# Linear attention's root ahead of the first half's exponentials on ScalarE, its output ahead of the second half's maximum on VectorE

## The chip, the cores and the metric

The kernel runs on one core of one Trainium2 chip. The metric is the device time of one execution in microseconds (us); less is better. Of a kernel that is timed several times the median is given.

## The reference

One decoder layer: 1024 tokens, width 1024, batch 1, float32. One projection feeds two groups of heads; their outputs are joined, projected and added, and an MLP follows. The part that the change touches is the work on one block of 128 tokens:

```
# head group A: sliding window attention, 8 heads of 64
s = einsum(q, k2) * dh**-0.5 + bias            # 128 queries, 256 keys
m = max(max(s), sink);  p = exp(s - m)
p = p / (sum(p) + exp(sink - m));  o = p @ v2
# head group B: chunked gated linear attention, 4 heads, keys 64, values 128
A = where(causal, q_t @ k_t.T, 0)              # within a chunk of 64 tokens
o = A @ v + q_t @ S_prev;  S = decay * S + k_s.T @ v
o = rms_norm(o) * gla_norm_g;  gla = o * silu(g_out)
mix = concat([attn, gla]) @ w_out
```

## The kernel before

The program of each engine is written out by hand, in order, and semaphores tie them together; nothing reorders it. After the input projections comes the attention loop: 8 blocks of 128 tokens. Block 0 is written out, blocks 1 to 7 are the turns of a loop (`Fori(1, NT)` on VectorE, `Fori(1, NT - 1)` and one more `steady` on ScalarE, a Python loop on TensorE). The loop is pipelined: turn n makes scores and exponentials of block n and finishes attention and linear attention of block n - 1.

- TensorE (PE), turn n: `front(n, 0)` scores of heads 0 to 3 (L848); `probs_turned` twice, transposes of block n - 1's probabilities (L815); `front(n, 1)` scores of heads 4 to 7; `attend(n - 1)` (L826); first part of `g_out(n)`, 12 matmuls (L784); `gla_scores(n)` (L860); `out_turned(n - 1)`, which transposes `gla_out` (L834); `gla_keys(n)` (L869); second part of `g_out(n)`, 12 matmuls; `gla_out_of(n)`: products with keys (L893), with the mask `a_mask` (L902), with `state_a` and `state_b` (L913).
- VectorE (DVE), turn n: `scores(n, 0)`, which moves two score tiles out of PSUM (L1330) and takes maximum, negated maximum and sink difference (L1336 to L1338); `gla_variance` (L1375); `gla_next_state` (L1381); `scores(n, 1)`; `gla_finish`, a Newton step on the root (L1123 to L1126) and the four products that make `gla_out` (L1391); `normalise(n, 0)` (L1344, L1345 and four L1347); `mix_attn` and `mix_gla`, the low halves of the joined output (L1353); `gla_mask` (L1358); `normalise(n, 1)`; `gla_state_b` (L1366).
- ScalarE (ACT), turn n: `turned` twice (L1820, L1822); `gla_squares` (L1842); `sigmoid` (L1859); `exps(n, 0)`, four exponentials and one of the sinks (L1827, L1828); `gla_root`, logarithm and exponential of 4 columns (L1728, L1729); `mix_hi` of the attention part (L1836); `exps(n, 1)`; `mix_hi` of the linear attention part; `keys` (L1832); `silu_exp` (L1851 to L1854).
- GpSimd (POOL): after `silu_exp`, a low part (L585) and a sum (L588); after `sigmoid`, the product that makes the gate `silu_g` (L590), for which `gla_finish` waits.

The waits that matter: `exps(n, g)` waits for the sink difference of that half (semaphore `neg_max`), `gla_finish` for root and gate, `out_turned` for `gla_out`, the second `mix_hi` for `out_turned`, `mix_gla` for the second `mix_hi`, and `gla_out_of` for mask and keys. Nothing on the way has a second buffer that could take up a late step.

Of the kernel before, what the change touches and what calls it, by code (L numbers as in the profile page):

```python
# [152 lines left out]
def build(nc, x, c, w_ada, b_ada, w_in, w_gate_up, b_gate, gla_norm_g, attn_sinks, rel_bias,  # L153
# [222 lines left out]
    with block:  # L376
# [717 lines left out]
        def _(v):  # L1094
# [16 lines left out]
            def split_lo(s, par):  # L1111
                v.wait_ge(s_hi, s + 1)
                v.tensor_tensor(w_lo[:, par, :], raw[:, par, :], w_hi[:, par, :], ALU.subtract).then_inc(s_lo, 1)  # L1113
# [7 lines left out]
            def newton(y, vv, t):  # L1121

                own.link(v.tensor_tensor(t, y, y, ALU.mult))  # L1123
                own.link(v.tensor_tensor(t, t, vv, ALU.mult))
                own.link(v.tensor_scalar(t, t, -0.5, 1.5, ALU.mult, ALU.add))
                return v.tensor_tensor(y, y, t, ALU.mult)  # L1126
# [195 lines left out]
            def scores(n, g, first=False):  # L1322

                for j in range(2):
                    hp = 2 * g + j
                    v.wait_ge(s_sc_full, 4 * n + hp + 1)
                    if not first and j == 0:
                        v.wait_ge(s_pt_full, 4 * (n - 1) + 2 * g + 2)
                    lo = P if first else 0
                    v.scalar_tensor_tensor(prob[:, 2 * hp:2 * hp + 2, lo:256],  # L1330
                                           bank[hp % 2][:, :].rearrange("p (h k) -> p h k", h=2)[:, :, lo:256],
                                           DH ** -0.5, bias[:, 2 * hp:2 * hp + 2, lo:256], ALU.mult, ALU.add)\
                        .then_inc(s_sc_free, 1)
                h = slice(4 * g, 4 * g + 4)
                v.wait_ge(s_sc_free, 4 * n + 2 * g + 2)
                own.link(v.tensor_reduce(mx[:, h], prob[:, h, :], AX.X, ALU.max))  # L1336
                own.link(v.scalar_tensor_tensor(nm[:, h], mx[:, h], -1.0, n_sink[:, h], ALU.mult, ALU.min))
                v.tensor_tensor(sd[:, h], nm[:, h], n_sink[:, h], ALU.subtract).then_inc(s_nm, 1)  # L1338

            def normalise(n, g):  # L1340

                h = slice(4 * g, 4 * g + 4)
                v.wait_ge(s_exp, 2 * n + g + 1)
                own.link(v.tensor_tensor(den[:, h], rs[:, h], es[:, h], ALU.add))  # L1344
                own.link(v.reciprocal(den[:, h], den[:, h]))  # L1345
                for i in range(4 * g, 4 * g + 4):
                    ins = v.tensor_scalar(prob[:, i, :], prob[:, i, :], den[:, i:i + 1], None, ALU.mult)  # L1347
                ins.then_inc(s_pn, 1)
# [6 lines left out]
            def gla_mask(n):  # L1355

                for hh in range(2):
                    ins = v.copy_predicated(a_mask[:, hh:GLA_HEADS:2, :],  # L1358
                                            tri[:, :].bitcast(I32).unsqueeze(1).broadcast_to([P, 2, P]),
                                            bank[(5, 7)[hh]][:, 0:2 * P].rearrange("p (h q) -> p h q", h=2))  # L1360
                ins.then_inc(s_at, 1)

            def gla_state_b(n):
                v.wait_ge(s_ds_full, n + 1)
                for tt in range(2):
                    ins = v.scalar_tensor_tensor(state_b[:, tt, :], state_a[:, tt, :], dec(n, 0, tt),  # L1366
                                                 bank[5][:, tt * P:(tt + 1) * P], ALU.mult, ALU.add)
                ins.then_inc(s_st_b, 1)
# [4 lines left out]
            def gla_variance(n):  # L1373
                v.wait_ge(s_gsq, n + 1)
                v.tensor_scalar(gvar, gss, 1.0 / DV, EPS, ALU.mult, ALU.add).then_inc(s_gvar, 1)  # L1375

            def gla_next_state(n):

                v.wait_ge(s_st_b, n + 1)
                for tt in range(2):  # L1380
                    ins = v.scalar_tensor_tensor(state_a[:, tt, :], state_b[:, tt, :], dec(n, 1, tt),  # L1381
                                                 bank[7][:, tt * P:(tt + 1) * P], ALU.mult, ALU.add)
                ins.then_inc(s_st_a, 1)

            def gla_finish(n):

                v.wait_ge(s_sg, n + 1)
                v.wait_ge(s_grt, n + 1)
                own.link(newton(grs, gvar, gnt))
                for h in range(GLA_HEADS):  # L1390
                    ins = v.scalar_tensor_tensor(gla_out[:, h, :], bank[(6, 4)[h % 2]][:, h // 2 * P:(h // 2 + 1) * P],  # L1391
                                                 grs[:, h:h + 1], silu_g[:, h * DV:(h + 1) * DV], ALU.mult, ALU.mult)
                ins.then_inc(s_og, 1)

            def mix_attn(n):
                mix(act_lo[:, 0:4, ds(n * P, P)], act_hi[:, 0:4, ds(n * P, P)], bank[2], s_oa_hi, n + 1, s_oa_lo)

            def mix_gla(n):
                mix(act_lo[:, 4:8, ds(n * P, P)], act_hi[:, 4:8, ds(n * P, P)], bank[4], s_gt_hi, n + 1, s_gt_lo)

            scores(0, 0, first=True)
            split_lo(SLOT_T + 3, (SLOT_T + 1) % 2)
            scores(0, 1, first=True)
            v.wait_ge(s_at_full, 1)
            gla_mask(0)
            normalise(0, 0)
# [7 lines left out]
            with v.Fori(1, NT, 1) as n:  # L1414
                own.enter(n - 1, LINKS)
                scores(n, 0)
                gla_variance(n - 1)
                gla_next_state(n - 1)
                scores(n, 1)
                gla_finish(n - 1)  # L1420
                normalise(n, 0)
                mix_attn(n - 1)
                v.wait_ge(s_at_full, n + 1)
                mix_gla(n - 1)
                gla_mask(n)
                normalise(n, 1)
                gla_state_b(n)
                own.leave(NT - 1)
# [279 lines left out]
        def _(a):  # L1708
# [17 lines left out]
            def root(y, vv, t):  # L1726

                own.link(a.activation(t, vv, ACT.Ln))  # L1728
                return a.activation(y, t, ACT.Exp, scale=-0.5)  # L1729
# [87 lines left out]
            def turned(n, g):  # L1817

                a.wait_ge(s_pt_full, 4 * n + 2 * g + 1)
                a.activation(prob_t[:, g, 0, :], bank[2][:, :], ACT.Copy).then_inc(s_pt_2, 1)  # L1820
                a.wait_ge(s_pt_full, 4 * n + 2 * g + 2)
                a.activation(prob_t[:, g, 1, :], bank[3][:, :], ACT.Copy).then_inc(s_pt_3, 1)  # L1822

            def exps(n, g):
                a.wait_ge(s_nm, 2 * n + g + 1)
                for h in range(4 * g, 4 * g + 4):
                    a.activation(prob[:, h, :], prob[:, h, :], ACT.Exp, bias=nm[:, h:h + 1], accum_out=rs[:, h:h + 1])  # L1827
                a.activation(es[:, 4 * g:4 * g + 4], sd[:, 4 * g:4 * g + 4], ACT.Exp).then_inc(s_exp, 1)  # L1828
# [5 lines left out]
            def mix_hi(tiles, n, b, wait, done):  # L1834
                a.wait_ge(wait, n + 1)
                a.activation(act_hi[:, tiles, ds(n * P, P)], b[:, :].rearrange("p (t q) -> p t q", t=4), ACT.Copy)\  # L1836
                    .then_inc(done, 1)

            def gla_squares(n):
                a.wait_ge(s_go_full, n + 1)  # L1840
                for h in range(GLA_HEADS):
                    ins = a.activation(gla_out[:, h, :], bank[(6, 4)[h % 2]][:, h // 2 * P:(h // 2 + 1) * P],  # L1842
                                       ACT.Square, accum_out=gss[:, h:h + 1])
                ins.then_inc(s_gsq, 1)
# [11 lines left out]
            def sigmoid(n):  # L1856

                a.wait_ge(s_sg_sum, n + 1)
                a.activation(silu_g[:, :], silu_g[:, :], ACT.Exp, scale=-1.0).then_inc(s_sigmoid, 1)  # L1859

            def gla_root(n):
                a.wait_ge(s_gvar, n + 1)
                root(grs, gvar, gln).then_inc(s_grt, 1)
# [5 lines left out]
            def steady(n):  # L1869
                turned(n - 1, 0)  # L1870
                turned(n - 1, 1)
                gla_squares(n - 1)
                sigmoid(n - 1)
                exps(n, 0)
                gla_root(n - 1)
                mix_hi(slice(0, 4), n - 1, bank[2], s_oa_full, s_oa_hi)
                exps(n, 1)
                mix_hi(slice(4, 8), n - 1, bank[4], s_gt_full, s_gt_hi)
                keys(n)
# [244 lines left out]
```

## Time and profile before

| | before |
|---|---|
| median of 3 runs | 1111.54 us (1108.22 to 1111.82) |
| profiled execution, its own time | 1111.64 us |
| its span in the profile | 1109.5 us |
| TensorE busy | 1039.9 us, 94% |
| VectorE busy | 702.4 us, 63% |
| ScalarE busy | 462.9 us, 42% |
| GpSimd busy | 94.3 us, 8% |
| one turn of the loop, 302.14 to 319.22 | 17.08 us: TensorE 16.11 busy, VectorE 13.58, ScalarE 12.04, GpSimd 4.47 |

The span is the time from the first to the last instruction on the chip; the 2.1 us between it and the execution's time lie around it. Busy is the time in which at least one instruction of an engine runs. In the loop all engines hand work to one another within a turn, so that what counts is who waits for whom, and not the share alone. The granted clock of TensorE is 1.00 in the turn.

### The profile page before, as it was taken

What the parts mean: (1) busy time and instruction counts of PE and PEld (TensorE: products, weight loads), DVE (VectorE), ACT (ScalarE), POOL (GpSimd) and SP (SyncE); (2) the same over time, 40 slices, a digit from 0 to 9 for tenths busy, and PEclk for the clock granted to TensorE, in tenths of its full rate; (3) what the DMA queues carried; (4) which work ended last, traced back from release to release, by engine and by line L of the source; (5) the groups of instructions that cost most, each with busy time, mean ns of one, the idle gap of its engine ahead of it and who ended that gap; (6) DMA issues with size and microseconds to landing.
All of it is one profiled execution on the core that took longest, in us unless ns stands there. A gap on an engine that the chain in (4) does not pass through costs nothing.

```text
span 1109.5 us, 12725 instructions
## 1 busy us (share of the span) xinstructions
PE 1039.9 (94%) x4963; PEld 832.3 (75%) x4963; DVE 702.4 (63%) x895; ACT 462.9 (42%) x717; POOL 94.3 (8%) x119
## 2 busy tenths in 40 slices
PE   1699999989999999989999999999989999999995
PEld 1578884866666788777888888888878888888884
DVE  6766663677787542698565565545448944477567
ACT  1641001356677511566545444555334243424342
POOL 0002210012223200000000000000122000001100
PEclk9999999999999999999999999999999999999998
DMA  9918751010000442315543354416897423454623
GB/s 351 306 52 295 240 174 38 1 39 1 1 1 1 150 116 76 152 39 172 189 172 131 133 174 147 173 57 246 316 359 273 147 81 114 152 209 157 222 77 152
DMA packets 87618, 163.17 MB, mean 147 GB/s; under 512 B 15267, under 2 KB 36236, under 8 KB 87564
## 3 DMA queue, kind: packets, MB, share of 16 engines
q1 hardware_dynamic: 75740, 119.90, 31.3%
q0 software_dynamic: 11824, 42.51, 10.7%
q8 instruction: 39, 0.64, 0.2%
q14 instruction: 15, 0.12, 0.0%
HBM read 124.63 MB, written 37.76 MB: 146 GB/s over the span
## 4 chain that ended last, share of the span: by engine, by line
PE 78%; DVE 12%; ACT 4%; DMA 2%; issue 2%; SPq 2%; DVEq 0%; ACTq 0%
PE bank L1029 24%; PE bank L1048 24%; PE bank L784 13%; PE bank L654 10%; DMA x_in<-in_x 1%; PE bank L749 1%; DVE small L1336 1%; DVE prob L1330 1%; DVE x L1650 1%; PE bank L815 1%; PE bank L848 1%; DVE h_lo_T L1486 1%; DMA hid_raw<-hidden_forms 1%; ACT gla_out L1842 1%; PE bank L913 1%
## 5 line engine op out<-in xcount | busy, mean ns | idle before, releaser
L1048 PE MATMUL bank<-dn_hi,hid_hi 128*128 128x512 f32 x448 | 175.1, 391 | 3.5 <-DVE dn_lo L1576 3.5
L1048 PE MATMUL bank<-dn_hi,hid_lo 128*128 128x512 f32 x448 | 175.2, 391 | 0.0
L1048 PE MATMUL bank<-dn_lo,hid_hi 128*128 128x512 f32 x448 | 175.0, 391 | 0.0
L1573 DVE TENSOR_TENSOR hid_lo<-hid_raw,hid_hi 128x2048 fp32r<-128x2048 f32 x28 | 64.1, 2290 | 115.3 <-ACT hid_hi L2010 115.3
L2010 ACT ACTIVATE hid_hi<-hid_raw 128x2048 fp32r<-128x2048 f32 x28 | 53.6, 1915 | 169.7 <-PE bank L1048 154.0
L784 PE MATMUL bank<-w_hi,act_hi 128*128 128x512 f32 x256 | 102.3, 400 | 0.9 <-DVE w_lo L1113 0.9
L1029 PE MATMUL bank<-h_hi_T,up_hi 128*128 128x512 f32 x256 | 100.0, 391 | 1.6 <-DVE h_lo_T L1486 1.5
L1048 PEld LDWEIGHTS bank<-dn_hi,hid_hi 128*128 128x128 f32 x448 | 84.5, 189 | 21.6 <-DVE dn_lo L1576 3.9
L1446 DVE TENSOR_TENSOR up_lo<-up_raw,up_hi 128x1024 fp32r<-128x1024 f32 x48 | 58.7, 1223 | 65.4 <-ACT up_hi L1915 65.4
L784 PE MATMUL bank<-w_lo,act_hi 128*128 128x512 f32 x256 | 99.9, 390 | 0.0
L784 PE MATMUL bank<-w_hi,act_lo 128*128 128x512 f32 x256 | 99.8, 390 | 0.0
L1029 PE MATMUL bank<-h_hi_T,up_lo 128*128 128x512 f32 x256 | 99.7, 389 | 0.0
L1029 PE MATMUL bank<-h_lo_T,up_hi 128*128 128x512 f32 x256 | 99.7, 389 | 0.0
L1048 PEld LDWEIGHTS bank<-dn_lo,hid_hi 128*128 128x128 f32 x448 | 84.5, 189 | 17.5
L1048 PEld LDWEIGHTS bank<-dn_hi,hid_lo 128*128 128x128 f32 x448 | 84.4, 188 | 17.5
L1724 ACT ACTIVATE w_hi<-raw 128x2048 fp32r<-128x2048 f32 x13 | 24.9, 1915 | 141.3 <-PE bank L654 91.9
L1915 ACT ACTIVATE up_hi<-up_raw 128x1024 fp32r<-128x1024 f32 x48 | 50.5, 1057 | 76.5 <-PE bank L1029 57.6
L1029 PE MATMUL bank<-h_hi,up_hi 128*128 128x512 f32 x192 | 75.8, 395 | 4.4 <-ACT hid L1993 2.5
L1029 PE MATMUL bank<-h_hi,up_lo 128*128 128x512 f32 x192 | 75.5, 393 | 0.0
L1029 PE MATMUL bank<-h_lo,up_hi 128*128 128x512 f32 x192 | 75.3, 392 | 0.0
L654 PE MATMUL bank<-act_hi,w_hi 128*128 128x512 f32 x160 | 63.2, 395 | 0.4 <-issue 0.4
L654 PE MATMUL bank<-act_lo,w_hi 128*128 128x512 f32 x160 | 62.4, 390 | 0.0
(225 smaller groups left out, 1875.3 us busy)
## 6 DMA issues: line engine op xcount, KB each, us to landing
hidden_forms<-hid SPq DMA_DIRECT2D x56, 512.0 KB, 3.3
hid_raw<-hidden_forms SPq DMA_DIRECT2D x56, 512.0 KB, 4.4
ada_w<-in_w_ada POOLq DMA_DIRECT2D x32, 512.0 KB, 6.6
up_raw<-in_w_mlp_in SPq DMA_DIRECT2D x32, 512.0 KB, 5.3
dn_ring<-in_w_mlp_out POOLq DMA_DIRECT2D x24, 512.0 KB, 4.9
raw<-in_w_in SPq DMA_DIRECT2D x36, 256.0 KB, 5.0
ada_w_first<-in_w_ada SPq DMA_DIRECT2D x8, 1024.0 KB, 10.7
dn_t<-in_w_mlp_out POOLq DMA_DIRECT2D x16, 512.0 KB, 7.0
```

Of the source, the lines that this page charges most:

```text
L654: mm = pe.matmul(bank[2 * half + m][:, :], w, act(b)[:, k, half * HALF:half * HALF + HALF], start=(n == 0), stop=(n == 3 * KT - 1))
L749: mm = pe.matmul(bank[half][0:RANK, :], (z_lo if a else z_hi)[:, k, :], act(b)[:, k, half * HALF:half * HALF + HALF], start=(n == 0), stop ...
L784: mm = pe.matmul(b, tok_act(i, 4 * part + k, t), wsl(j, s % 2)[:, k * HALF:(k + 1) * HALF], start=(part == 0 and n == 0), stop=(part == 1 ...
L815: mm = pe.transpose(bank[2 + kb][:, h * P:(h + 1) * P], prob[:, 4 * g + h, kb * P:(kb + 1) * P], ident[:, :])
L848: mm = pe.matmul(bank[g][:, j * 256:j * 256 + 256], q, k_t[g * DH:(g + 1) * DH, n * P:(n + 2) * P], start=True, stop=True)
L1029: mm = pe.matmul(b, (up_hi, up_lo)[x][f % 4][:, k, m * P:(m + 1) * P], (h_hi, h_lo)[y][name][:, k, :], start=(UP_STARTS[i] and n == 0), st ...
L1048: mm = pe.matmul(b, (hid_hi, hid_lo)[x][n % 2][:, k, t * P:(t + 1) * P], (dn_hi, dn_lo)[y][n % 2][:, k, :], start=(first and i == 0), stop ...
L1446: v.tensor_tensor(up_lo[f % 4][:, :, :], up_form(f), up_hi[f % 4][:, :, :], ALU.subtract).then_inc(s_wlo, 1)
L1573: v.tensor_tensor(hid_lo[n % 2][:, :, :], hid_raw[n % 2][:, :, :], hid_hi[n % 2][:, :, :], ALU.subtract)\
L1724: a.activation(w_hi[:, par, :], raw[:, par, :], ACT.Copy).then_inc(s_hi, 1)
L1915: a.activation(up_hi[f % 4][:, :, :], up_form(f), ACT.Copy).then_inc(s_whi, 1)
L2010: a.activation(hid_hi[n % 2][:, :, :], hid_raw[n % 2][:, :, :], ACT.Copy).then_inc(s_dhi, 1)
```

## The change

On ScalarE `gla_root(n - 1)` moves ahead of `exps(n, 0)`. On VectorE the last three instructions of `scores` become a function of their own, `largest`; it follows `scores` at once everywhere but for the second half in the loop, where `gla_finish(n - 1)` now stands between the two. No instruction is added or removed. TensorE, GpSimd and the DMA queues keep their order.

```diff
                         .then_inc(s_sc_free, 1)
+            def largest(n, g):
+
                 h = slice(4 * g, 4 * g + 4)
                 v.wait_ge(s_sc_free, 4 * n + 2 * g + 2)
                 own.link(v.tensor_reduce(mx[:, h], prob[:, h, :], AX.X, ALU.max))
...
                 scores(n, 0)
+                largest(n, 0)
                 gla_variance(n - 1)
                 gla_next_state(n - 1)
                 scores(n, 1)
                 gla_finish(n - 1)
+                largest(n, 1)
                 normalise(n, 0)
...
                 sigmoid(n - 1)
+                gla_root(n - 1)
                 exps(n, 0)
-                gla_root(n - 1)
                 mix_hi(slice(0, 4), n - 1, bank[2], s_oa_full, s_oa_hi)
```

VectorE, in the loop, from the second score tile of the second half (L1330) to the first instruction of `normalise`. Before:

```order
L1330 SCALAR_TENSOR_TENSOR prob<-bank,bias 128x512 [waits scores_full]
L1336 TENSOR_REDUCE small<-prob 128x4 [waits scores_read]
L1337 SCALAR_TENSOR_TENSOR small<-small 128x4 [waits vector_own]
L1338 TENSOR_TENSOR small<-small 128x4 [waits vector_own]
L1123 TENSOR_TENSOR small<-small 128x4 [waits gla_root,silu_ready]
L1124 TENSOR_TENSOR small<-small 128x4 [waits vector_own]
L1125 TENSOR_SCALAR small<-small 128x4 [waits vector_own]
L1126 TENSOR_TENSOR small<-small 128x4 [waits vector_own]
L1391 SCALAR_TENSOR_TENSOR gla_out<-bank,small,silu_g 128x128 [waits vector_own]
L1391 SCALAR_TENSOR_TENSOR gla_out<-bank,small,silu_g 128x128 x3
L1344 TENSOR_TENSOR small<-small 128x4 [waits exps]
```

After the change (the lines past the new function are numbered two higher):

```order
L1330 SCALAR_TENSOR_TENSOR prob<-bank,bias 128x512 [waits scores_full]
L1123 TENSOR_TENSOR small<-small 128x4 [waits gla_root,silu_ready]
L1124 TENSOR_TENSOR small<-small 128x4 [waits vector_own]
L1125 TENSOR_SCALAR small<-small 128x4 [waits vector_own]
L1126 TENSOR_TENSOR small<-small 128x4 [waits vector_own]
L1393 SCALAR_TENSOR_TENSOR gla_out<-bank,small,silu_g 128x128 [waits vector_own]
L1393 SCALAR_TENSOR_TENSOR gla_out<-bank,small,silu_g 128x128 x3
L1338 TENSOR_REDUCE small<-prob 128x4 [waits scores_read]
L1339 SCALAR_TENSOR_TENSOR small<-small 128x4 [waits vector_own]
L1340 TENSOR_TENSOR small<-small 128x4 [waits vector_own]
L1346 TENSOR_TENSOR small<-small 128x4 [waits exps]
```

The eight instructions of `gla_finish` have moved up past the three of the second half's maximum.

ScalarE, in the loop, from `sigmoid` to the first `mix_hi`. Before:

```order
L1859 ACTIVATE silu_g<-silu_g 128x512 [waits silu_summed]
L1827 ACTIVATE prob,small<-prob,small 128x256 [waits neg_max]
L1827 ACTIVATE prob,small<-prob,small 128x256 x3
L1828 ACTIVATE small<-small 128x4
L1728 ACTIVATE small<-small 128x4 [waits gla_variance]
L1729 ACTIVATE small<-small 128x4 [waits scalar_own]
L1836 ACTIVATE act_hi<-bank 128x4x128
```

After the change (lines numbered six higher):

```order
L1865 ACTIVATE silu_g<-silu_g 128x512 [waits silu_summed]
L1734 ACTIVATE small<-small 128x4 [waits gla_variance]
L1735 ACTIVATE small<-small 128x4 [waits scalar_own]
L1833 ACTIVATE prob,small<-prob,small 128x256 [waits neg_max]
L1833 ACTIVATE prob,small<-prob,small 128x256 x3
L1834 ACTIVATE small<-small 128x4
L1842 ACTIVATE act_hi<-bank 128x4x128
```

The two instructions of the root have moved up past the five of the first half's exponentials.

## Rows read from the trace of the kernel before

**Rows 1.** TensorE's waits: line, who released it, us in total, times, longest

```profile
PE bank L834 <- DVE gla_out L1391: 4.9, 7, 0.9
PE bank L913 <- DVE state_b L1366: 1.8, 1, 1.8
```

**Rows 2.** The chain that ended last: start us, us, what

```profile
309.44 1.23 DVE small L1336
...
369.73 2.21 DVE w_lo L1113
371.99 3.03 PE bank L784 x12
```

**Rows 3.** Timeline of TensorE, turn four: start, us; idle before in brackets

```profile
301.56 0.65 PE L913 MATMUL bank<-state_b,gq_t 64*64 64x128 f32 x8
...
312.95 0.66 PE L834 MATMUL bank<-ident,gla_out 128*128 128x128 f32 x4 [0.63 <-DVE gla_out L1391]
...
316.52 0.68 PE L893 MATMUL bank<-gv_tok,gks_tok 64*64 64x128 f32 x16
...
318.64 0.66 PE L913 MATMUL bank<-state_b,gq_t 64*64 64x128 f32 x8
```

**Rows 4.** Timeline of VectorE, turn four

```profile
304.33 1.29 DVE L1330 SCALAR_TENSOR_TENSOR prob<-bank,bias 128x512 f32<-128x512 f32 x2 [2.83 <-PE bank L815]
...
308.12 1.28 DVE L1330 SCALAR_TENSOR_TENSOR prob<-bank,bias 128x512 f32<-128x512 f32 x2
...
310.89 0.17 DVE L1338 TENSOR_TENSOR small<-small 128x4 f32<-128x4 f32 x1
310.97 0.17 DVE L1123 TENSOR_TENSOR small<-small 128x4 f32<-128x4 f32 x1
...
311.77 1.12 DVE L1391 SCALAR_TENSOR_TENSOR gla_out<-bank,small,silu_g 128x128 f32<-128x128 f32 x4
312.81 0.15 DVE L1344 TENSOR_TENSOR small<-small 128x4 f32<-128x4 f32 x1
...
314.27 1.28 DVE L1353 TENSOR_TENSOR act_lo<-bank,act_hi 128x512 f32 x2
315.46 0.77 DVE L1358 COPY_PREDICATED a_mask<-tri,bank 128x256 f32<-128x256 int32 x2
...
316.53 1.54 DVE L1347 TENSOR_SCALAR prob<-prob,small 128x256 f32<-128x256 f32 x4
317.99 0.59 DVE L1366 SCALAR_TENSOR_TENSOR state_b<-state_a,small,bank 128x128 f32<-128x128 f32 x2
```

**Rows 5.** Timeline of ScalarE, turn four

```profile
309.76 0.22 ACT L1828 ACTIVATE small<-small 128x4 f32<-128x4 f32 x1
309.85 0.22 ACT L1728 ACTIVATE small<-small 128x4 f32<-128x4 f32 x1
...
310.21 0.59 ACT L1836 ACTIVATE act_hi<-bank 128x512 f32 x1
311.09 0.51 ACT L1827 ACTIVATE prob<-prob,small 128x256 f32<-128x256 f32 x1 [0.28 <-DVE small L1338]
...
313.07 0.19 ACT L1828 ACTIVATE small<-small 128x4 f32<-128x4 f32 x1
313.74 0.60 ACT L1836 ACTIVATE act_hi<-bank 128x512 f32 x1 [0.48 <-PE bank L834]
...
316.63 0.60 ACT L1851 ACTIVATE g_copy<-bank 128x512 f32<-128x512 f32 x1 [2.02 <-PE bank L784]
```

**Rows 6.** Timeline of GpSimd, turn four

```profile
308.01 1.29 POOL L590 TENSOR_TENSOR silu_g<-g_copy,silu_g 128x512 f32<-128x512 f32 x1 [4.51 <-ACT silu_g L1859]
317.31 1.92 POOL L585 TENSOR_SCALAR g_low<-g_copy 128x512 f32<-128x512 f32 x1 [8.01 <-ACT g_copy L1851]
```

**Rows 7.** Timeline of GpSimd ahead of the first turn

```profile
246.45 3.45 POOL L585 TENSOR_SCALAR g_low<-g_copy 128x512 f32<-128x512 f32 x1 [11.96 <-ACT g_copy L1851]
249.99 1.26 POOL L588 TENSOR_TENSOR silu_g<-silu_g,g_low 128x512 f32<-128x512 f32 x1
```

**Rows 8.** Timeline of VectorE, single products of `normalise`, ahead of the first turn

```profile
249.09 0.95 DVE L1347 TENSOR_SCALAR prob<-prob,small 128x256 f32<-128x256 f32 x2
...
249.97 1.43 DVE L1347 TENSOR_SCALAR prob<-prob,small 128x256 f32<-128x256 f32 x1
```

**Rows 9.** The same in turn four: the last product

```profile
317.32 0.75 DVE L1347 TENSOR_SCALAR prob<-prob,small 128x256 f32<-128x256 f32 x1
```

More of the change, by code:

```diff
@@ L1401, in _ @@
             scores(0, 0, first=True)
+            largest(0, 0)
             split_lo(SLOT_T + 3, (SLOT_T + 1) % 2)
             scores(0, 1, first=True)
+            largest(0, 1)
             v.wait_ge(s_at_full, 1)
```

## Prediction

> **What bounds the kernel now.** I read the page first: TensorE is busy for 94% of the span, so only its waits can be saved outright. Its list of waits [rows 1] shows what the loop has to offer: 4.9 us in 7 waits for `gla_out`, one a turn. (`state_b` makes it wait once, ahead of the first turn.) This is the wait that the change goes for, and at 0.7 us a turn it is all there is.
>
> Then the timeline of a turn, engine by engine. TensorE's product with `state_b` starts at 301.56 and again at 318.64, so a turn takes 17.08 us [rows 3]. In it TensorE waits 0.63 us for `gla_out`, ahead of L834. VectorE waits 2.83 us for the transposes at the start of its turn, at 304.33, and from there its rows follow one another to the end of `state_b` at 317.99 + 0.59 = 318.58 [rows 4]. TensorE's last product starts at 318.64, 0.06 us behind that. So two chains end together: TensorE's own work plus its one wait, and VectorE's 14.25 us of work, which begins when TensorE's transposes are done. The view of waits doesn't name `state_b`, since TensorE has just finished L913's first half; but there is hardly any slack. The chain that ended last runs through both, with the second half's maximum in it [rows 2].
>
> What follows for the change: taking 0.63 us out of TensorE brings nothing unless VectorE's end at 318.58 comes earlier too, and each new wait on VectorE is paid nearly in full.
>
> **The change part by part,** on the clock of turn four; primes mark the new times.
>
> *The root ahead of the exponentials.* Root to next instruction is 310.21 - 309.85 = 0.36 us [rows 5]. The root's input, `gla_variance`, is made before `scores(n, 1)`, so it stands ready when `sigmoid` is done. The first half's exponentials end 0.36 us later, at about 310.1 + 0.2; the attention `mix_hi` stays at 310.21, since the same work lies ahead of it. `normalise(n, 0)` wants these exponentials at 312.81 [rows 4]. Cost nothing; without that cover of 2.5 us it would be 0.36.
>
> *The output ahead of the maximum.* `gla_finish` needs the root (done by 308.3') and the gate, which GpSimd has ready at 308.01 + 1.29 = 309.30 [rows 6]. VectorE is through with L1330 at 309.40 [rows 4], so `gla_finish'` starts at 309.44, where the maximum did [rows 2]: no wait. It takes 312.81 - 310.97 = 1.84 us until the next instruction; its last product ends at 309.44 + 0.80 + 1.12 = 311.36'. TensorE comes to L834 at 312.95 - 0.63 = 312.32 [rows 3]. The wait is gone with 1 us to spare: TensorE is 0.63 us ahead.
>
> *What is late instead: the second half's maximum.* It starts at 309.44 + 1.84 = 311.28'. From its start to L1338 is 310.89 - 309.44 = 1.45, and ScalarE's exponentials start 0.20 after L1338 [rows 4, 5]: 312.93', 1.84 later than 311.09. Behind them on ScalarE are queued the linear attention's `mix_hi`, `keys` and `silu_exp`. The exponentials take 313.07 + 0.09 - 311.09 = 2.07 us (0.09 from L1828 to L1728), so `mix_hi` starts at 315.00' and ends at 315.60', where before it started at 313.74, having waited for TensorE [rows 5]. The head start on L834 is of no use to it any more.
>
> *Who waits for that.* VectorE itself. Its three instructions and `gla_finish` have only changed places, so `normalise(n, 0)` starts at 312.81 as before and `mix_attn` at 314.27. `mix_gla` would start (315.46 - 314.27) / 2 = 0.60 later, at 314.87, but has to wait for 315.60' plus a few hundredths: 315.62'. A new wait of **0.75 us**. Behind it are queued mask, `normalise(n, 1)` and `state_b`, all 0.75 us later. The mask ends at 315.46 + 0.77 + 0.75 = 316.98'; TensorE, which could start L893 at 316.52 - 0.63 = 315.89', waits some 1.1 us and starts at about 317.0', 0.5 later than before. (The keys are ready by 315.9' and don't decide.) Its `state_b` product could then start at 319.12', but `state_b` is ready only at 318.58 + 0.75 = 319.33': start at 319.39'. The turn is **0.75 us** longer. Next turn's transposes, and with them VectorE's start, hang on that point.
>
> *What GpSimd does to it.* `normalise(n, 1)` shares its time with GpSimd's L585. Four products take 1.54 us instead of some 1.15, because the last, which starts with L585 at 317.32, takes 0.75 [rows 6, 9]. The change moves the two apart: `silu_exp` follows TensorE's earlier end and starts at 316.00', so L585 at 316.68', while the products start at 317.28'. Where would they meet? Ahead of the first turn L585 is held up and its own 1.92 us lie from 247.98 to 249.90. A product 1.11 us into it, at 249.09, is not hindered; the next starts some 1.37 us into it and ends at 250.04 [rows 7, 8]. In the new turn the third product starts 1.13 us into L585 and the fourth 1.4: the fourth is held until about 318.74', as much as before. `state_b'` then ends at 319.25 to 319.33. Bounds: without any hold the products save 0.4 and TensorE's own 0.5 us remain; how much a worse meeting costs is a rival below.
>
> The Trainium skill (SBUF — State Buffer, Who interferes with whom) says that VectorE and GpSimd share a port pair as an exclusive lock, which the first to issue holds for its whole instruction. The row disagrees in part: L585 runs until 319.23, but the product that starts 0.01 us behind it ends at 318.07 [rows 6, 9]. By the rule all four products would wait for L585's end at 318.60', and the turn would be about 1.7 us longer (estimated from these rows), 1123.5 in all.
>
> *The ends of the loop.* Seven turns have this form. After the last, TensorE waits for `w_lo`, which VectorE makes right behind `state_b` [rows 2]; so the shift of the last turn is passed on whole. From there on TensorE has its work in a row, later stages hang on it, and I find nothing that would absorb the delay.
>
> Sum: 7 x 0.75 = 5.25 us. The profiled execution took 1111.64 us, within 0.1 of the median, so **1116.9 us**, 0.5% slower.
>
> **The rivals.**
> - *Forecast, the wait moves to VectorE's `mix_gla` (0.62).* With 0.5 to 1.0 us a turn (TensorE's own shift; or a product or `state_b` held 0.25 longer): 1115.1 to 1118.6.
> - *The change hardly counts (0.16).* The 1.8 us that the exponentials slip are partly made good, say since the products meet no GpSimd and TensorE catches up with the state at once: 0.2 to 0.45 us a turn, 1113 to 1114.8. For it speaks that 0.75 is a small difference of large terms; against it that each term has its row.
> - *Faster (0.10).* The second `mix_hi` is done by the time VectorE wants it, so no wait takes the old one's place, and the products clear L585: TensorE's 0.63 us a turn less the part that VectorE sets, at most 0.4, so 2.8 us less, 1108.8; with all 0.63, 1107.2. It decides at 314.87: exponentials and copy would have to be 0.75 us of 2.67 shorter. Nothing in the rows suggests it.
> - *Worse meeting with GpSimd (0.12).* If L588 gets in front of the fourth product, as it did ahead of the first turn, where that took 1.43 us [rows 8], it is held until L588' is through: 318.68 + 1.26 + 0.15 = 320.1', `state_b` ends at 320.6', 2.0 us a turn: 1125.6. The third product at 1.13 us into L585 against 1.37, where one was held, is what keeps it off. The lock of the Trainium skill would act in this direction.
>
> **How the numbers follow.** The predicted time is the forecast's. The range of 1111.5 to 1120.5 holds the forecast and "hardly counts", and leaves out most of "faster" and "worse meeting", 2 in 10. Within 0.3% (3.3 us), about what a measurement of this kernel can tell from no change, are the second case and a little of the others: 0.19. Faster by more: 0.07. Slower by more: the forecast and the bad meeting, 0.74.
>
> **What would show it.** In the changed kernel's profile: TensorE's 7 waits for `gla_out` are gone; in their place stand 7 of about 1.1 us ahead of L893 for the mask, and possibly some tenths ahead of the `state_b` product; VectorE idles some 0.75 us ahead of the second low-half subtraction, released by ScalarE's `act_hi`; ScalarE waits over 2 us ahead of the second half's exponentials instead of 0.28; a turn takes 17.8 us. I am wrong if `mix_gla` finds its input ready, or if the four products of `normalise(n, 1)` take far from 1.5 us.

## The result, and the profile after

The changed kernel takes 1122.08 us (median of 6 runs, 1119.78 to 1124.29), the kernel before 1111.42 (6 runs, 1108.22 to 1112.57): a ratio of 1.0103, 95% interval 1.0086 to 1.0120. It is slower by 1%, twice what was forecast and above the range. The profiled execution has a span of 1122.1 us against 1109.5.

TensorE's waits in the changed kernel (line, releaser, us in total, times, longest):

```profile
PE bank L893 <- DVE a_mask L1360: 8.9, 7, 1.3
PE bank L913 <- DVE state_b L1368: 8.5, 7, 1.8
```

The 7 waits for `gla_out` of [rows 1] are gone. In their place stand 7 for the mask, 1.27 us each, and 6 more for `state_b` than before, 1.1 us each. (The one of 1.8 us is the old one ahead of the first turn.)

VectorE at the end of turn three and in turn four, to be read against [rows 4]; all times from the span's start:

```profile
302.68 0.69 DVE L1355 TENSOR_TENSOR act_lo<-bank,act_hi 128x512 f32 x1 [0.82 <-ACT act_hi L1842]
303.29 0.76 DVE L1360 COPY_PREDICATED a_mask<-tri,bank 128x256 f32<-128x256 int32 x2
303.95 0.23 DVE L1346 TENSOR_TENSOR small<-small 128x4 f32<-128x4 f32 x1
304.21 0.18 DVE L1347 RECIPROCAL small<-small 128x4 f32<-128x4 f32 x1
304.42 2.57 DVE L1349 TENSOR_SCALAR prob<-prob,small 128x256 f32<-128x256 f32 x4
306.92 0.60 DVE L1368 SCALAR_TENSOR_TENSOR state_b<-state_a,small,bank 128x128 f32<-128x128 f32 x2
310.35 1.29 DVE L1330 SCALAR_TENSOR_TENSOR prob<-bank,bias 128x512 f32<-128x512 f32 x2 [2.83 <-PE bank L815]
...
315.34 0.16 DVE L1123 TENSOR_TENSOR small<-small 128x4 f32<-128x4 f32 x1
...
316.14 1.13 DVE L1393 SCALAR_TENSOR_TENSOR gla_out<-bank,small,silu_g 128x128 f32<-128x128 f32 x4
...
318.62 0.17 DVE L1340 TENSOR_TENSOR small<-small 128x4 f32<-128x4 f32 x1
```

Two things differ. `mix_gla` (L1355) waits 0.82 us for the second `mix_hi`; and the four products of `normalise(n, 1)` (L1349) take 2.57 us where they took 1.54. The sum ahead of them (L1346) takes 0.23 us, where it took 0.15. ScalarE's row says why `mix_hi` is late: ahead of the second half's exponentials ScalarE stands idle for 2.00 us, until the maximum's last instruction (L1340) is done. Before it was 0.28 us [rows 5].

```profile
318.82 0.51 ACT L1833 ACTIVATE prob<-prob,small 128x256 f32<-128x256 f32 x1 [2.00 <-DVE small L1340]
```

TensorE, and then GpSimd, in the same stretch:

```profile
304.11 0.69 PE L893 MATMUL bank<-gv_tok,gks_tok 64*64 64x128 f32 x16 [1.28 <-DVE a_mask L1360]
...
307.57 0.65 PE L913 MATMUL bank<-state_b,gq_t 64*64 64x128 f32 x8 [1.10 <-DVE state_b L1368]
```

```profile
303.55 1.95 POOL L585 TENSOR_SCALAR g_low<-g_copy 128x512 f32<-128x512 f32 x1 [7.27 <-ACT g_copy L1857]
305.58 1.26 POOL L588 TENSOR_TENSOR silu_g<-silu_g,g_low 128x512 f32<-128x512 f32 x1
```

The products one by one (narrow windows of the same timeline; the middle row is the third alone):

```profile
304.69 0.95 DVE L1349 TENSOR_SCALAR prob<-prob,small 128x256 f32<-128x256 f32 x2
304.95 0.69 DVE L1349 TENSOR_SCALAR prob<-prob,small 128x256 f32<-128x256 f32 x1
305.57 1.43 DVE L1349 TENSOR_SCALAR prob<-prob,small 128x256 f32<-128x256 f32 x1
```

The third starts 1.40 us into L585 and is held until that is over, 0.69 us instead of 0.35. So the fourth comes at 305.57, together with L588 at 305.58, and is held for the whole of it: 1.43 us. It is the picture of [rows 7, 8], now in turns 1 to 6.

Where the time lies: `state_b` marks the end of a turn on VectorE. Differences of its starts, in us, from the timelines:

| | turn 1 | turns 2 to 6, each | turn 7 | from block 0 to block 7 |
|---|---|---|---|---|
| before (247.90 to 369.14) | 18.91 | 17.05 | 17.05 | 121.24 |
| after (249.77 to 381.89) | 19.05 | 19.04 | 17.87 | 132.12 |

The loop takes 10.9 us more; the medians are 10.7 apart. (The two profiled executions are 12.6 apart. Of that, 1.9 us lie ahead of the loop, where the two kernels do the same work, and where the profiles of all 14 versions spread by 4 us.) Before, turn 1 is no good measure: in this execution TensorE ran from 248.56 to 251.60 at a granted clock of 0.51, behind its 1.8 us wait; in the profile of root_alone below, with the clock up, the turn takes 17.37 us. Against that one, turn 1 of the changed kernel is 1.7 us longer. Turn 7 of the changed kernel is the useful exception. There ScalarE copies `w_hi` ahead of `silu_exp`, L585 starts only with the fourth product, and the products take 1.49 us:

```profile
378.80 0.69 DVE L1355 TENSOR_TENSOR act_lo<-bank,act_hi 128x512 f32 x1 [0.81 <-ACT act_hi L1842]
...
380.47 1.49 DVE L1349 TENSOR_SCALAR prob<-prob,small 128x256 f32<-128x256 f32 x4
```

```profile
381.21 1.92 POOL L585 TENSOR_SCALAR g_low<-g_copy 128x512 f32<-128x512 f32 x1 [8.81 <-ACT g_copy L1857]
```

The wait is the same, the turn 0.82 us longer than before instead of 1.99. So the kernel itself holds both cases side by side.

### The profile page after: what moved, and what is told of

It is laid out like the page before. It is cut to its first block, busy times and chain, and to the rows that moved or that the text cites. A ratio compares the mean times of both kernels' runs of the same rounds, so it can differ in the third digit from the quotient of the medians.

```text
span 1122.1 us, 12725 instructions
## 1 busy us (share of the span) xinstructions
PE 1042.3 (93%) x4963; PEld 832.3 (74%) x4963; DVE 709.7 (63%) x895; ACT 461.9 (41%) x717; POOL 94.4 (8%) x119
## 4 chain that ended last, share of the span: by engine, by line
PE 74%; DVE 14%; ACT 5%; issue 3%; DMA 2%; SPq 1%; DVEq 0%; ACTq 0%
PE bank L1029 24%; PE bank L1048 23%; PE bank L784 12%; PE bank L654 10%; DMA x_in<-in_x 1%; ACT prob L1833 1%; DVE prob L1349 1%; PE bank L749 1%; DVE small L1338 1%; DVE x L1656 1%; PE bank L815 1%; DVE h_lo_T L1492 1%; DMA hid_raw<-hidden_forms 1%; DVE prob L1330 1%; DVE gla_out L1393 1%
## 5 line engine op out<-in xcount | busy, mean ns | idle before, releaser
L1048 PEld LDWEIGHTS bank<-dn_hi,hid_lo 128*128 128x128 f32 x448 | 84.4, 188 | 17.8
```

The source lines that it names most:

```text
L1048: mm = pe.matmul(b, (hid_hi, hid_lo)[x][n % 2][:, k, t * P:(t + 1) * P], (dn_hi, dn_lo)[y][n % 2][:, k, :], start=(first and i == 0), stop ...
```

## The experiments

Two parts of the loss were to be told apart: the wait of `mix_gla`, and the meeting of the products with GpSimd. Ratios are to the kernel before, timed again with each set of experiments (medians 1110.4, 1110.2 and 1111.8 us), with 95% intervals; "turn" is the distance of `state_b` in turns 2 to 6.

**GpSimd held back** (the change, and then the kernel before, each with this edit):

```diff
                 pool.wait_ge(s_g_copy, n + 1)
+                pool.wait_ge(s_st_b, n + 1)
```

> The changed kernel, with GpSimd's low part and sum (L585, L588) held back until the turn's state_b is made, so that they can no longer meet the products of normalise(n, 1). Theory 'wait and meeting': the four products take 1.14 us again instead of 2.57, the 0.8 us wait of mix_gla stays, the mask still makes TensorE wait about 1.2 us, and TensorE's own path behind the mask sets the turn: 17.6 to 17.7 us instead of 19.03, in all some 1115.5 us. Rival 'the wait is everything': the products' length is hidden behind other work, the turn stays near 19 us, 1122. Rival 'the meeting is everything': the turn falls back to 17.05, 1111.

Measured 1112.9 us, ratio 1.0023 (1.0012 to 1.0033), turn 17.53 us. The wait stays, the products are back at 1.14:

```profile
316.65 0.69 DVE L1356 TENSOR_TENSOR act_lo<-bank,act_hi 128x512 f32 x1 [0.82 <-ACT act_hi L1843]
...
318.32 1.14 DVE L1350 TENSOR_SCALAR prob<-prob,small 128x256 f32<-128x256 f32 x4
```

Both rivals fall: the turn gives back 1.5 of the 2.0 us with the meeting gone, and keeps 0.5. This is not yet the split of the loss, since the kernel before has a meeting too, which holds its last product [rows 9]; the next run gives the other half.

> The kernel before with the same delay of GpSimd as in the first run of this set. The last product of normalise(n, 1) takes 0.35 us instead of 0.75, so VectorE's end of the turn comes 0.4 us earlier. Theory 'two chains end together': TensorE's own work and its 0.63 us wait for gla_out still make the turn, 17.05 us, 1111.4, no change. Rival: VectorE's chain alone sets the turn, which then falls by 0.4 us, 1108.6.

Measured 1108.3 us, ratio 0.9983 (0.9971 to 0.9995), turn 16.69 us. Here my theory falls and the rival holds. TensorE waits for `gla_out` as long as before, and yet the turn is 0.36 us shorter:

```profile
PE bank L835 <- DVE gla_out L1392: 4.9, 7, 0.9
```

```profile
298.39 0.33 PE L914 MATMUL bank<-state_a,gq_t 64*64 64x128 f32 x2
298.45 0.33 PE L914 MATMUL bank<-state_b,gq_t 64*64 64x128 f32 x2
```

The second fence is TensorE's timeline in turn three. With `state_b` ready, the products with `state_a` and with `state_b` run in pairs, 0.06 us apart; in [rows 3] the latter starts at 318.64, behind all eight of the former, which began at 318.22. TensorE had lost 0.4 us there, and no view named it.

The two runs together split the loss. Without a meeting in either kernel the change costs 17.53 - 16.69 = 0.84 us a turn; that is the wait, and agrees with the 0.82 of turn 7. The meeting costs 19.04 - 17.53 = 1.51 us in the changed kernel and 17.05 - 16.69 = 0.36 before, so it is worse by 1.15.

**ScalarE's part alone, and VectorE's part alone:**

```diff
# root_alone: the kernel before, ScalarE      # finish_alone: the changed kernel, ScalarE
+                gla_root(n - 1)              -                gla_root(n - 1)
                 exps(n, 0)                                    exps(n, 0)
-                gla_root(n - 1)              +                gla_root(n - 1)
```

> The kernel before with ScalarE's part of the change alone: the root ahead of the first half's exponentials. Theory: nobody waits for either earlier, since the first half's exponentials have 2.5 us of slack and gla_finish still stands behind the maximum; turn 17.05 us, 1111.4, within 0.3%. Rival: the 0.36 us that the exponentials slip are paid, 7 times, 1114.

Measured 1109.52 us, ratio 0.9996 (0.9986 to 1.0006), turn 17.07 us. The root's place by itself costs and gives nothing.

> The changed kernel with the root back behind the first half's exponentials: VectorE's part alone. Theory: gla_finish now waits about 1 us for the root on VectorE, everything behind it (maximum, second exponentials, second mix_hi, mask, state_b) is that much later than in the changed kernel, so a turn takes 1 us more than there wherever the products meet GpSimd as badly (20.0 us, 1129), or 18.7 us (1123) if the later start clears them. Rival: VectorE's order alone carries the loss and the root's place does not matter, 1122.

Measured 1132.24 us, ratio 1.0199 (1.0184 to 1.0214), turns of 20.1 to 20.5 us. `gla_finish` waits for the root, on VectorE:

```profile
317.77 0.17 DVE L1123 TENSOR_TENSOR small<-small 128x4 f32<-128x4 f32 x1 [1.02 <-ACT small L1735]
```

The products meet GpSimd as badly (2.62 us), so the theory's first case holds: from VectorE's start of the turn to `state_b` it is 16.66 us (311.69 to 328.35 in turn four) against 15.60 in the changed kernel, the 1 us that was expected. The turns are 0.1 to 0.4 us longer still, and that lies between `state_b` and VectorE's next start: 2.92 to 3.23 us of idle time instead of 2.83. There TensorE works at the lower clock. In every turn it waits 2.2 us for the mask, and behind each of these waits its granted clock falls to 0.50 for over 3 us, so that its products with the mask take 2.02 us instead of 1.16. TensorE's waits, its clock in a stretch behind one (window, us, busy, granted clock, DMA share, GB/s), and then its products and VectorE's next start:

```profile
PE bank L893 <- DVE a_mask L1360: 15.3, 7, 2.2
```

```profile
305.90:309.20 3.30, 3.30 (x22) 0.50 0.01 2
```

```profile
305.78 2.02 PE L902 MATMUL bank<-gv_tok,a_mask 128*128 128x128 f32 x8
```

```profile
311.69 1.29 DVE L1330 SCALAR_TENSOR_TENSOR prob<-bank,bias 128x512 f32<-128x512 f32 x2 [3.15 <-PE bank L815]
```

**The moment of the meeting.** A short instruction on GpSimd ahead of L585, first one of 0.11 us, then one of 0.53:

```diff
                 pool.wait_ge(s_g_copy, n + 1)
+                if n > 0:
+                    pool.memset(c_exp, 0.0)
```

```diff
                 pool.wait_ge(s_g_copy, n + 1)
+                if n > 0:
+                    pool.memset(g_low[:, :], 0.0).then_inc(s_pool, 1)
+                    pool.wait_ge(s_pool, 2 * n)
...
-                pool.wait_ge(s_pool, n + 1)
+                pool.wait_ge(s_pool, 2 * n + 1)
```

> The changed kernel with one more tiny instruction on GpSimd, ahead of L585 in each turn: it sets eight columns to zero that nothing reads any more. Its length d is not known; it moves L585 later by d and changes nothing else. In the changed kernel the third product of normalise(n, 1) starts 1.41 us into L585 and is held, and the fourth is caught by L588. Theory 'the moment decides': with d above 0.1 and under about 0.8 us the third product starts less than 1.3 us into L585 and passes, the four products take some 1.5 us instead of 2.57, and the turn falls to 17.8 to 17.9 us, in all 1117 (5 us less for more work). Rival: the products are slowed by GpSimd's work as such, wherever it lies, and the turn stays at 19.03, 1122.

Measured 1122.41 us, ratio 1.0109 (1.0092 to 1.0125), turn 19.08. It settled nothing but showed a coupling. GpSimd, then VectorE:

```profile
303.68 0.11 POOL L586 MEMSET small<- 128x8 f32 x1 [7.25 <-ACT g_copy L1859]
303.75 1.95 POOL L587 TENSOR_SCALAR g_low<-g_copy 128x512 f32<-128x512 f32 x1
```

```profile
304.10 0.28 DVE L1348 TENSOR_TENSOR small<-small 128x4 f32<-128x4 f32 x1
304.42 0.18 DVE L1349 RECIPROCAL small<-small 128x4 f32<-128x4 f32 x1
304.63 2.57 DVE L1351 TENSOR_SCALAR prob<-prob,small 128x256 f32<-128x256 f32 x4
```

The main instruction (L585, here L587) starts only 0.07 us behind the tiny one, and the small sum ahead of the products, which reads two tiles of SBUF, was itself held (0.28 us against 0.15 in [rows 4], 0.23 in the changed kernel). So the products start 0.88 us into GpSimd's instruction here and 0.87 in the changed kernel: in this stretch they follow it.

> The changed kernel with an instruction of some 0.53 us on GpSimd ahead of L585 in each turn (it clears the tile that L585 writes next), so L585 starts 0.6 us later. The tiny one before it moved L585 by 0.07 us only, and the products moved with it: the small sum ahead of them (L1346) took 0.28 us instead of 0.15. Theory 'the moment decides': L585 now starts behind that small sum, the first product starts some 0.2 us into L585 and is held for 0.3 to 0.5 us, the other three pass and are through before L588: the four take 1.5 us instead of 2.57, a turn 17.6 to 17.9 us, 1116 to 1118, for more work on GpSimd. Rival 'GpSimd's share as such': 19 us and 1122.

Measured 1116.73 us, ratio 1.0039 (1.0024 to 1.0054), turn 17.73. GpSimd, then VectorE:

```profile
317.54 0.53 POOL L586 MEMSET g_low<- 128x512 f32 x1 [7.25 <-ACT g_copy L1860]
318.16 2.01 POOL L588 TENSOR_SCALAR g_low<-g_copy 128x512 f32<-128x512 f32 x1
```

```profile
317.97 0.15 DVE L1349 TENSOR_TENSOR small<-small 128x4 f32<-128x4 f32 x1
...
318.37 1.33 DVE L1352 TENSOR_SCALAR prob<-prob,small 128x256 f32<-128x256 f32 x4
```

With more work on GpSimd the kernel is 5 us faster than the changed one. The sum is free again and the products, which start 0.21 us into GpSimd's instruction, take 1.33 us. It is the moment that decides, not GpSimd's load. The turn is about as long as the prediction had drawn it (17.8), though here the first product is held (0.55 us) and there it was the last.

**`state_b` ahead of `normalise(n, 1)`,** on the changed kernel and on the kernel before:

```diff
                 gla_mask(n)
+                gla_state_b(n)
                 normalise(n, 1)
-                gla_state_b(n)
```

> The changed kernel with state_b made ahead of normalise(n, 1) on VectorE, so that TensorE no longer waits for the products, however long they take. Theory 'wait and meeting': of the 1.98 us a turn only TensorE's wait for the mask stays; it starts L893 some 0.6 us later than before, but runs its two state products side by side, as it did when GpSimd was held back, and wins 0.4 of that: a turn of 17.2 to 17.3 us, 1112 to 1113, with the products still 2 us and longer. Rival: the products' length is paid elsewhere, at the second transposes of the next turn, 18 us and more, 1118.

Measured 1115.74 us, ratio 1.0051 (1.0036 to 1.0066), turn 17.31.

> The kernel before with state_b ahead of normalise(n, 1) on VectorE. With GpSimd held back it fell to 16.69 us a turn, since TensorE then ran its two state products side by side; it had waited 0.4 us for state_b without the view of waits naming it. Theory 'hidden wait for state_b': the same here without touching GpSimd, 16.69 us a turn, 1108 to 1109. Rival: it was GpSimd's delay itself, for instance for the copies that feed gla_finish, and the turn stays at 17.05, 1111.

Measured 1112.25 us, ratio 1.0016 (1.0006 to 1.0026), turn 16.68.

Both turns are what the theory gave, to 0.05 us, and the second confirms the hidden wait without touching GpSimd. Neither time is. The loss lies behind the loop: TensorE now waits for `w_lo`, which VectorE makes behind the last `normalise` (TensorE's waits of before_state_first; there were 0.9 us before):

```profile
PE bank L784 <- DVE w_lo L1113: 3.7, 2, 3.3
```

and then runs slower. Its clock around that wait, which ends at 370.18 (columns as above): 0.50 of 2.4 GHz is the lower level, 1.2 GHz.

```profile
366.00:370.00 4.00, 0.85 (x8) 1.00 0.00 0
370.90:374.20 3.30, 3.30 (x10) 0.50 0.00 0
374.30:378.00 3.70, 3.70 (x21) 1.00 0.35 107
```

From TensorE's last product with `state_b` to the end of the span it is 743.9 us, and 739.3 in the kernel before: 4.6 us, of which the wait is 2.8.

**The second `mix_hi` and `keys` ahead of the second exponentials,** alone, and with `state_b` moved up:

```diff
-                exps(n, 1)
                 mix_hi(slice(4, 8), n - 1, bank[4], s_gt_full, s_gt_hi)
                 keys(n)
+                exps(n, 1)
```

> The changed kernel with ScalarE's second mix_hi and keys ahead of the second half's exponentials, and nothing else. Theory: mix_gla's wait of 0.82 us is gone, mask and products stand where they stood before; L585 starts about where the first product starts, so one product or two are held. VectorE alone sets the turn: 17.05 us if the four products take 1.5, 1111, up to 17.5 (1114) if L585 catches one more. Rival: the second exponentials, 0.8 us later than in the changed kernel, become the new wait, at normalise(n, 1), and the turn stays near 18, 1118.

Measured 1108.83 us, ratio 0.9973 (0.9962 to 0.9984), turn 16.98; the products take 1.49. This one edit to the changed kernel turns its loss of 1% into a gain of 0.3%. The wait of `mix_gla` is gone, so that wait was the root of both parts: L585 starts 12.23 us after VectorE's start of the turn, as in the changed kernel (12.24), but the products now start at 12.13 and not at 13.11, so that L585 and L588 no longer catch two of them one after the other. Of the gain I can place 0.8 us in turns 2 to 7 and 0.5 at `w_lo`, where TensorE waits 0.4 us instead of 0.9; the rest is open.

> The changed kernel with two moves: on ScalarE the linear attention's mix_hi and keys ahead of the second half's exponentials, on VectorE state_b ahead of normalise(n, 1). Theory: mix_gla finds its input ready (no wait of 0.8 us), the mask ends 316.23 - 304.33 = 11.9 us after VectorE's start of the turn as in the kernel before, TensorE waits 0.4 us for it instead of 1.3, its state products run side by side: a turn of 16.45 us, 1107, faster than before by 0.4%. Rival: the second exponentials, now 0.8 us later still, are late for normalise(n, 1) and the next turn's transposes, and the turn stays at 17 us, 1111.

Measured 1108.14 us, ratio 0.9982 (0.9971 to 0.9992), turn 16.40. The turn is right (TensorE waits 0.4 us for the mask, the second exponentials are nobody's wait), the sum is not: 4.5 us gained in the loop, 2 kept, and again TensorE waits behind the loop, 0.9 us for `silu_exp` and 1.1 for `w_lo`, and its granted clock is 0.50 from 365.2 to 368.5. There the profile is 2.9 us longer than that of the kernel before.

**The tail, and the head:** the last turn of VectorE's loop written out, with

```diff
                 gla_state_b(n)
+                if isinstance(n, int):
+                    split_lo(SLOT_O, SLOT_O % 2)
                 normalise(n, 1)
```

> The version with mix_hi and state_b moved up (16.40 us a turn, yet only 2 us less than before in all), with the last turn of VectorE's loop written out so that w_lo of the output projection is made ahead of the last normalise. Theory: what the loop gained was lost behind it, where TensorE waited for w_lo and then ran twelve matmuls at half its clock; now w_lo is ready some 1.5 us earlier relative to state_b, and the clock stays up: 3 us less than that version, 1105 against 1110.2 for the kernel before. Rival: the last normalise is late for TensorE's second transposes instead and the gain is lost once more, 1108.

Measured 1105.69 us, ratio 0.9941 (0.9927 to 0.9955), turn 16.41. The wait for `w_lo` is down to 0.4 us, and the clock behind the loop is 1.00 (363.00 to 380.00):

```profile
PE bank L784 <- DVE w_lo L1113: 0.4, 1, 0.4
```

This is the fastest version found, 0.6% ahead of the kernel before and 1.6% ahead of the changed one.

> The same, and ahead of the loop state_b and the second normalise of block 0 before the gating of an output slot (2.3 us). Theory: TensorE's one wait of 1.8 us for state_b ahead of the first turn is gone: 1.8 us less than the run beside it, 1103. Rival: the gating, now between the products and the first scores, is late for the first turn, 1105.

Its edit puts `gla_state_b(0)` and `normalise(0, 1)` ahead of `gate_out_slot`. Measured 1106.07 us, ratio 0.9946 (0.9933 to 0.9959): no further gain, the rival holds. The 1.8 us wait is gone, but turn 1 has become 17.88 us, since the gating now delays its first scores:

```profile
253.90 1.14 PE L848 MATMUL bank<-k_t,q_t 64*128 64x256 f32 x8 [0.93 <-DVE prob L1330]
```

## Why the prediction was wrong

- *The root costs nothing; the output is made without a wait; TensorE's wait for it goes.* Right. `gla_finish` starts 4.99 us after VectorE's start of the turn (315.34 - 310.35), against 5.11 forecast, and the 7 waits are gone; root_alone shows the cover of the first exponentials.
- *The wait moves to `mix_gla`, 0.75 us.* Right, 0.82 measured (the second exponentials slip by 1.71 us, 1.84 forecast), and turn 7, which has only this, is 0.82 us longer. That this wait starts the whole loss was shown by after_hi_first, where moving the copy (and the keys behind it) on ScalarE removes it.
- *TensorE waits 1.1 us for the mask.* Right, 1.27.
- *What GpSimd does to it.* This step failed. The prediction put the third product 1.13 us into L585, free to pass as one had at 1.11, and the fourth at 1.4, held as much as before. Measured are 1.40 for the third and 2.02 for the fourth, which so falls to L588: 2.57 us for four products instead of 1.5. With the later start this is 1.2 us a turn (19.04 against 17.87 in turn 7), six times. Counted from VectorE's start of the turn, L585 came 0.12 us earlier than forecast (TensorE was through with `g_out` that much sooner) and the first product 0.16 us later: 0.09 with the mask, the rest since the sum ahead of the products is itself held by L585's start. The prediction had not seen that tie. It put the first product 0.60 us into L585, and measured are 0.87, in turns 1 to 6 alike.
- The rival "worse meeting with GpSimd" is what came: its mechanism to the row (the fourth held until L588 is through, 1.43 us), its turn at 2.0 us against 1.99 measured. It had a chance of 0.12 because the meeting was judged by one point, 1.13 against a row at 1.11, while its neighbour at 1.37 lay within the sum's own error. Its total of 1125.6 took seven bad turns where there were six. Six at 1.99 us and one at 0.82 would make 12.8 us, and the medians are 10.7 apart; in the profiles 1.5 us of the difference is turn 1 of the kernel before, long there by its lower clock (18.91 against 17.37), and the 1111.64 us from which the prediction counted are those of that execution. Whether the other executions divide the same way no trace shows.
- *The lock of the Trainium skill.* The Trainium skill (SBUF — State Buffer, Who interferes with whom) has the loser of the shared port pair blocked for the other's whole instruction. For L588 the rows agree: the product ends at 307.00, 0.16 us behind L588. For L585 they don't: two products pass in its midst. As a rough rule it would have pointed to the right side of the forecast, though its 1.7 us a turn came from another picture.
- *Two chains end together, TensorE's own 0.5 us as the floor.* Half right. VectorE alone set the turn; TensorE had 0.4 us in hand at its state products (before_pool_late, before_state_first: 16.69 and 16.68). So TensorE's floor was lower than I had it: with GpSimd held back the changed kernel is 0.48 us a turn behind the kernel before, where TensorE's waits alone (1.27 us for the mask, less 0.70 for `gla_out`) would give 0.57.
- *Nothing behind the loop absorbs or adds.* For the change itself right: TensorE's wait for `w_lo` is 0.52 us in both. Not so for the experiments that shortened the loop, where the tail took back 2.9 us (after_hi_state) and 4.6 us (before_state_first).

## What to carry to other kernels

When an instruction is moved ahead of another on one engine, follow the one that is made late through every queue that it passes: here a maximum slipped by 1.7 us, and a copy that was queued behind its exponentials on ScalarE came back to VectorE as a wait. The same copy moved ahead of them made the idea pay. And where two engines share an access, work out the moment at which their instructions meet with its error in both directions; if a neighbouring case lies within that error, it deserves a large share of the chance, since what it costs (1.2 us a turn) can be larger than what the change moves (0.8).

## What the runs showed of the hardware

- A matrix product on a 64 x 64 part of the array can run beside one on another part: eight with `state_a` and eight with `state_b` start in pairs 0.02 to 0.06 us apart where both inputs are ready, and take 0.4 us less together. The Trainium skill (TensorEngine Tiling (Array Packing), Key Properties) says that different tiles work in parallel; the view of waits doesn't show what it costs when one input is late, since the engine is busy with the other.
- GpSimd's `tensor_scalar` of 128x512 (1.92 us alone, 2.0 when met) holds VectorE's products near its start and near its end, not in between. A product of 0.35 us takes 0.55 to 0.75 us when it starts within 0.2 us of L585's start, 0.35 when it starts 0.67 to 1.20 us into it, and 0.69 to 0.77 when it starts 1.30 to 1.41 us into it (all versions together, where L585 takes 1.9 to 2.0 us). GpSimd's `tensor_tensor` (1.26 us) holds throughout: a product that starts with it takes 1.43 us, one that starts 0.37 us into it 1.05 (after_state_first). VectorE's small sums with two inputs in SBUF are held too (0.15 to 0.28 us).
- A wait can cost TensorE more than its own length. Behind one of 3.3 us the granted clock was 0.50 for over 3 us of work (before_state_first), and so it was behind each of seven of 2.2 us (finish_alone). Behind the one of 1.8 us ahead of the first turn it fell in some profiles (before, after_hi_first) and not in others (the changed kernel, root_alone). Behind the changed kernel's waits of 1.28 and 1.10 us it stayed at 1.00.
